# RMS norm of eight attention heads: one root and one reciprocal of 8 by 512 for all heads, spread by matmuls

## The reference

```python
def rmsnorm(x, g):
    xf = x.astype(jnp.float32)
    y = xf * lax.rsqrt(jnp.mean(xf * xf, axis=-1, keepdims=True) + EPS)
    return (y * g.astype(jnp.float32)).astype(x.dtype)

def diff_attention(q, k, v, lam, subln_g, lam_init):
    ...
        p = jax.nn.softmax(sc - slopes * dist, axis=-1)
        a = p[:, :, 0] - lam * p[:, :, 1]
        return jnp.einsum('bhqk,bkhe->bqhe', a.astype(v.dtype), v)
    ...
    o = jnp.moveaxis(o, 0, 1).reshape(b, s, DA_HEADS, DA_V_DIM)
    o = rmsnorm(o, subln_g) * (1.0 - lam_init)
    return o.reshape(b, s, DA_V_W)

def hybrid_layer(...):
    ...
    mk, mv = jnp.split(m @ w_mem_kv, 2, axis=-1)
    o_xa = memory_attention(xa_q..., mk..., mv...)
    ...
    merged = (gate[:, :, 0] * (o_da @ w_da_o)
              + gate[:, :, 1] * (o_wa @ w_wa_o)
              + gate[:, :, 2] * (o_xa @ w_xa_o))
```

## Time and profile before

| | |
|---|---|
| profiled execution | 2739.36 us |
| its span, first to last instruction | 2737.6 us |
| mean granted TensorE clock | 0.959 of full |
| busy: TensorE / weight load / VectorE / ScalarE / GpSimd | 2386.6 / 1581.4 / 948.2 / 497.2 / 1024.2 us |
| chain that ended last | TensorE 67%, DMA 13%, VectorE 12%, ScalarE 5%, issue 2% |
| HBM read | 523.56 MB, 192 GB/s over the span |
| GpSimd busy in slices 7 to 10 of 40 (the first layer's FFN) | 0.6, 0.8, 0.8, 0.8 |

### The profile page before, as it was taken

The page is one execution under the profiler, slowest core; times in us unless marked ns, Lnnn a source line. Parts: engine busy times, 40 slices in busy tenths (PEclk is TensorE's granted clock), DMA queues, the critical chain, the costliest instruction groups (busy, mean ns, idle before and its releaser), DMA issues.

```text
span 2737.6 us, 27015 instructions
## 1 busy us (share of the span) xinstructions
PE 2386.6 (87%) x11244; PEld 1581.4 (58%) x11244; DVE 948.2 (35%) x1323; ACT 497.2 (18%) x1067; POOL 1024.2 (37%) x497
## 2 busy tenths in 40 slices
PE   6999968999989988787899999599888888888886
PEld 4778837887878856565668887533323232332322
DVE  4664664555020156544732363401111101021012
ACT  2324222121010044454431010100000000000001
POOL 5444606888787744332538887200000000000000
PEclk9999989999999999898999999699999999999999
DMA  4211202322222210100213224489999999999996
GB/s 133 70 47 47 93 0 66 104 93 92 93 93 79 93 47 31 47 32 31 93 53 101 93 93 154 184 363 416 416 418 417 418 417 417 416 416 417 417 418 279
DMA packets 172341, 527.43 MB, mean 193 GB/s; under 512 B 9954, under 2 KB 92091, under 8 KB 139451
## 3 DMA queue, kind: packets, MB, share of 16 engines
q1 hardware_dynamic: 169008, 521.17, 49.1%
q10 hardware_dynamic: 3211, 4.51, 0.5%
HBM read 523.56 MB, written 2.10 MB: 192 GB/s over the span
## 4 chain that ended last, share of the span: by engine, by line
PE 67%; DMA 13%; DVE 12%; ACT 5%; issue 2%; ACTq 0%; POOL 0%; SPq 0%; DVEq 0%; POOLq 0%
PE ps L1298 9%; PE ps L1299 9%; PE ps L1300 9%; PE ps L1756 8%; PE ps L1729 7%; DMA hT<-in_w_exp_up 5%; PE ps L1451 4%; DMA arena<-in_w_exp_up 4%; DMA ring<-in_w_exp_up 4%; PE ps L1314 3%; PE ps L1315 2%; PE ps L1316 2%; PE ps L1690 2%; ACT arena L722 1%; PE ps L1714 1%
## 5 line engine op out<-in xcount | busy, mean ns | idle before, releaser
L457 POOL TENSOR_TENSOR w_hi<-ring,one 128x1024 fp32r<-128x1024 f32 x208 | 403.8, 1942 | 516.4 <-PE ps L1300 285.7
L460 POOL TENSOR_TENSOR w_lo<-ring,w_hi 128x1024 fp32r<-128x1024 f32 x222 | 543.4, 2448 | 58.0 <-ACT w_hi L773 41.6
L1298 PE MATMUL ps<-h_hi,w_hi 128*128 128x512 f32 x864 | 346.2, 401 | 8.4 <-DVE h_lo L880 5.8
L1300 PE MATMUL ps<-h_hi,w_lo 128*128 128x512 f32 x864 | 337.7, 391 | 0.0
L1299 PE MATMUL ps<-h_lo,w_hi 128*128 128x512 f32 x864 | 337.7, 391 | 0.0
L552 POOL TENSOR_TENSOR arena<-arena 128x512 f32<-128x512 f32 x8 | 8.4, 1048 | 834.6 <-PE ps L1702 796.8
L1729 PE MATMUL ps<-ring,arena 128*64 128x512 f32 x944 | 212.6, 595 | 42.6 <-DMA ring<-in_w_exp_up 41.8
L1729 PE MATMUL ps<-arena 128*64 128x512 f32 x848 | 191.9, 595 | 39.8 <-DMA arena<-in_w_exp_up 39.8
L1298 PEld LDWEIGHTS ps<-h_hi,w_hi 128*128 128x128 f32 x864 | 163.1, 189 | 50.4 <-DVE h_lo L880 6.7
L1299 PEld LDWEIGHTS ps<-h_lo,w_hi 128*128 128x128 f32 x864 | 163.2, 189 | 36.8 <-issue 4.3
L1300 PEld LDWEIGHTS ps<-h_hi,w_lo 128*128 128x128 f32 x864 | 162.9, 189 | 34.6
(11 more groups left out here) (297 smaller groups left out, 3903.4 us busy)
## 6 DMA issues: line engine op xcount, KB each, us to landing
arena<-in_w_exp_down SPq DMA_DIRECT2D x66, 1024.0 KB, 19.9
ring<-in_w_exp_gate SPq DMA_DIRECT2D x59, 1024.0 KB, 24.1
ring<-in_w_exp_up SPq DMA_DIRECT2D x59, 1024.0 KB, 25.4
arena<-in_w_exp_gate SPq DMA_DIRECT2D x53, 1024.0 KB, 21.8
arena<-in_w_exp_up SPq DMA_DIRECT2D x53, 1024.0 KB, 23.0
ring<-in_w_exp_down SPq DMA_DIRECT2D x52, 1024.0 KB, 22.0
ring<-in_w_in SPq DMA_DIRECT2D x34, 1024.0 KB, 5.1
ring<-in_ffn_w_up SPq DMA_DIRECT2D x22, 1024.0 KB, 5.1
```

Source lines behind the costliest of these rows:

```text
L457: nc.gpsimd.tensor_tensor(hi, w, one[:].unsqueeze(2).to_broadcast(list(w.shape)), ALU.mult).then_inc(w_high, 1)
L460: nc.gpsimd.tensor_tensor(lo, w, hi.bitcast(f32), ALU.subtract).then_inc(w_split, 1)
L1298: mm(o, w[0][:, k, :], h[0][:, k, 0:ntok], start=(k == 0), stop=False)
L1300: last = mm(o, w[1][:, k, :], h[0][:, k, 0:ntok], start=False, stop=(k == KT - 1))
```

## The change

The sum of squares is now gathered, not spread. `head_col` is 128 by 15 with one column of 1/128 in the middle, and a window of 8 columns from it has that column at place h. So the product of head h puts its mean on partition h of one 8 by 512 block in PSUM bank 4 and adds zero to the others; the eight heads accumulate into it. ScalarE takes one root of 8 by 512 when all eight are in, and VectorE one reciprocal of 8 by 512. Then TensorE spreads row h over 128 partitions by a product with column h of the identity, repeated 128 times (`norm_rows`), into banks 5 to 7 in turn, and VectorE's multiply reads it from PSUM. These eight products stand between the two halves of the value projection, the multiplies behind the copies of its first half. Memory attention now also waits for all eight multiplies. `mean128` and seven eighths of `ort` and `orr` are gone.

```diff
--- before.py
+++ after.py
@@ -63,9 +63,9 @@
         hT, hT_at = place(sb("hT", [P, KT, S]), KT * S)
         arena, arena_at = place(sb("arena", [P, ARENA]), ARENA)
         one = sb("one", [P, 1])
+        head_col = sb("head_col", [P, 15])
         ident = sb("ident", [P, P])
         mean64 = sb("mean64", [P, P])
-        mean128 = sb("mean128", [P, P])
         vec = sb("vec", [P, NVEC])
         wr = sb("wr", [P, KT, NE])
         epsb = sb("epsb", [P, 1])
@@ -161,7 +161,7 @@
         memt = ar(23040, 2, D)
         memn = ar(25088, 2, D)
         junkm = ar(12160, D)
-        osq, ort, orr = ar(8192, 2, S), ar(9216, 2, S), ar(10240, 2, S)
+        osq, ort, orr = ar(8192, 2, S), ar(9216, S)[0:DA_H], ar(9728, S)[0:DA_H]
         xa_q, mkT, mv = ar(18944, KT, S), ar(23040, KT, MEM), ar(25088, 2, D)
         o_xa = xa_q
         xa_p = ar(4096, 2, 4, MEM)
@@ -464,7 +464,8 @@
             nc.gpsimd.memset(ident[:], 0.0)
             nc.gpsimd.memset(mean64[:], 0.0)
             nc.gpsimd.memset(epsb[:], EPS)
-            nc.gpsimd.memset(mean128[:], 1.0 / 128)
+            link(nc.gpsimd.memset(head_col[:], 0.0))
+            nc.gpsimd.memset(head_col[:, 7:8], 1.0 / 128)
             link(nc.gpsimd.memset(mask[:], 0.0))
             link(nc.gpsimd.memset(selB[:], 0.0))
             nc.gpsimd.memset(mean64[0:64, 0:64], 1.0 / 64)
@@ -772,18 +773,13 @@
                 w = view(ring[:, c % RS, :])
                 A(w_hi[:, i % 2, :].rearrange("p (k n) -> p k n", k=w.shape[1]), w, F.Copy).then_inc(w_highA, 1)
 
-            for h in range(9):
-                if h < 8:
-                    if h >= 2:
-                        act.wait_ge(on_ps, h - 1)
-                    A(osq[:, h % 2, :], o_raw[:, h, :], F.Square).then_inc(on_sq, 1)
-                    high_part(by_act.start + h)
-                if h:
-                    m = h - 1
-                    act.wait_ge(on_ps, m + 1)
-                    if m >= 2:
-                        act.wait_ge(on_rr, m - 1)
-                    A(ort[:, m % 2, :], ps[:, 4 + m % 2, :], F.Sqrt, bias=epsb[:]).then_inc(on_rt, 1)
+            for h in range(8):
+                if h >= 2:
+                    act.wait_ge(on_ps, h - 1)
+                A(osq[:, h % 2, :], o_raw[:, h, :], F.Square).then_inc(on_sq, 1)
+                high_part(by_act.start + h)
+            act.wait_ge(on_ps, 8)
+            A(ort, ps[0:DA_H, 4, :], F.Sqrt, bias=epsb[0:DA_H]).then_inc(on_rt, 1)
             for i in by_act[8:]:
                 high_part(i)
             for u in range(XA_H + 1):
@@ -1115,22 +1111,19 @@
 
             norm(3, memt, memn)
             norm_lo(3, mem_lo, mem_hi, MEMG, MEM)
-            for h in range(9):
-                if h < 8:
-                    n = J_M + h
-                    dve.wait_ge(pj_ps, n + 1)
-                    V.tensor_copy(mkT[:, h, :], ps[:, h % 4, 0:MEM]).then_inc(pjD, 1)
-                if h:
-                    m = h - 1
-                    dve.wait_ge(on_rt, m + 1)
-                    V.reciprocal(orr[:, m % 2, :], ort[:, m % 2, :]).then_inc(on_rr, 1)
-                    dve.wait_ge(on_rr, m + 1)
-                    V.scalar_tensor_tensor(out=o_da[:, m, :], in0=o_raw[:, m, :], scalar=vec[:, SUBG:SUBG + 1],
-                                           in1=orr[:, m % 2, :], op0=ALU.mult, op1=ALU.mult).then_inc(on_done, 1)
+            for h in range(8):
+                dve.wait_ge(pj_ps, J_M + h + 1)
+                V.tensor_copy(mkT[:, h, :], ps[:, h % 4, 0:MEM]).then_inc(pjD, 1)
+            dve.wait_ge(on_rt, 1)
+            V.reciprocal(orr, ort).then_inc(on_rr, 1)
             for m in range(8, 12):
                 t, half = (m - 8) % 2, (m - 8) // 2
                 dve.wait_ge(pj_ps, J_M + m + 1)
                 V.tensor_copy(mv[:, t, half * 512:half * 512 + 512], ps[:, m % 4, :]).then_inc(pjD, 1)
+                for h in range(8) if m == 9 else ():
+                    dve.wait_ge(on_ps, 9 + h)
+                    V.scalar_tensor_tensor(out=o_da[:, h, :], in0=o_raw[:, h, :], scalar=vec[:, SUBG:SUBG + 1],
+                                           in1=ps[:, 5 + h % 3, :], op0=ALU.mult, op1=ALU.mult).then_inc(on_done, 1)
             for u in range(XA_H + 2):
                 if u < XA_H:
                     for qb in range(4):
@@ -1594,12 +1587,22 @@
             for h in range(8):
                 proj_T(1, (mem_hi, mem_lo), MEM)
                 pe.wait_ge(on_sq, h + 1)
-                if h >= 2:
-                    pe.wait_ge(on_rt, h - 1)
-                mm(ps[:, 4 + h % 2, :], mean128[:], osq[:, h % 2, :], start=True, stop=True).then_inc(on_ps, 1)
-            proj_tok((mem_hi, mem_lo), MEM // P, D)
+                mm(ps[0:DA_H, 4, :], head_col[:, 7 - h:15 - h], osq[:, h % 2, :], start=(h == 0), stop=(h == 7)).then_inc(on_ps, 1)
+
+            def norm_rows(h):
+
+                pe.wait_ge(on_rr, 1)
+                if h >= 3:
+                    pe.wait_ge(on_done, h - 2)
+                mm(ps[:, 5 + h % 3, :], ident[0:DA_H, h:h + 1].to_broadcast([DA_H, P]), orr, start=True, stop=True).then_inc(on_ps, 1)
+
+            proj_tok((mem_hi, mem_lo), MEM // P, 512)
+            for h in range(8):
+                norm_rows(h)
+            proj_tok((mem_hi, mem_lo), MEM // P, 512)
             pj_all_done(pe, J_M + 12)
-            pe.wait_ge(on_rt, 8)
+            pe.wait_ge(on_rt, 1)
+            pe.wait_ge(on_done, 8)
             for u in range(XA_H + 2):
                 if u < XA_H:
                     for qb in range(4):
```

## The result

The changed kernel takes 2742.28 us, the median of 17 runs (2733.19 to 2745.09). Beside them 17 runs of the kernel before gave 2738.11 (2730.46 to 2739.08). The ratio is 1.0020 with a 95% interval of 1.0012 to 1.0028: 4.2 us slower by the medians, 5.5 by the ratio, inside the 0.3% that I had called no change, but clear of the noise of so many runs. The forecast was 2737.0 in a range of 2729.5 to 2742.

A forecast was written before the change was run, and what follows sets the result against it. TensorE, waiting for weight halves held up by late reciprocals and roots, was taken to bound the stage. Half 12's readiness -7.2 us, eight products +6.1 (6.9 less 0.8): -1.1, from median 2738.11 to 2737.0; range 2729.5 to 2742.

The forecast's parts named there:

- the 0.3% that I had called no change: Whole kernel: about 0.3%, 8.2 us, is what a measurement can tell from no change; chance of landing within, 0.88.
- The wait of half 10 and the low clock behind it: Value weights' third half on TensorE: 6.05 us idle and 1.7 us of low clock go; it starts 5.4 us sooner.
- The sums of squares with 8 outputs cost nothing: Heads' sums on TensorE: 8 output rows instead of 128 change nothing, less than 0.1 us a head either way.
- The eight products in 6.9 us: Spreading products on TensorE between halves 11 and 12 of the weights: 0.86 us each, 6.9 us in all.
- No fall of the clock: TensorE up to memory attention: longest rest 0.6 us, so the granted clock stays at 1.00.
- The rival on the slower side: Spreading products filling 8 of 128 rows get 1.2 GHz: 13.8 us instead of 6.9, +7.5 us, 2745.6; chance 0.06.
- The slow multiplies: VectorE's eight multiplies: 2.5 to 2.9 us stalls beside GpSimd vanish with a PSUM operand; if stalled, end +0.7 instead of -1.1.
- It moves the end one for one: Stage before memory attention: everything behind waits for TensorE's counts, so what it gains or loses moves the end as much.
- The range: Whole kernel: 2729.5 to 2742 us, from the low figure to beyond the stalled multiplies, leaving out the clock's case.

The follow-up runs named there:

- e4: Kernel before, with ScalarE's high parts of halves 10 and 11 moved ahead of the roots of heads 6 and 7: 2727.61 us against 2736.43, ratio 0.9978; again 0.9973.
- e2: Changed kernel with only the sums of squares padded to 128 outputs, spreading products left at 8 partitions: 2742.47 us, ratio 1.0022 to before; stage 65.04 us.
- e7: Changed kernel with 64 outputs instead of 8 in the sums of squares; trace only: step of a head 4.06 us, stage 65.67 us.
- e3: Changed kernel with only the spreading products padded to 128 partitions, sums left at 8 outputs: 2737.16 us, ratio 1.0001 to before; stage 61.77 us.
- e5: Changed kernel with the spreading products over 64 partitions instead of 8; trace only: last sum to memory attention 33.98 us, stage 62.11 us.
- e6: Changed kernel with the spreading products over 32 partitions instead of 8; trace only: last sum to memory attention 38.85 us, stage 66.99 us.
- e1: Changed kernel with sums of squares and spreading products both padded to full 128: 2736.83 us against 2736.43 before, ratio 1.0010; stage 59.83 us.
- e8: Changed kernel with its eight spreading products two by two ahead of halves 12 to 15; trace only: last sum to memory attention 33.80 us, stage 61.94 us.

## Why the prediction was wrong

The forecast was a gain of 1.1 us; the stage lost 5.9.

- *The wait of half 10 and the low clock behind it* (13.0 us behind the last sum, to become 7.6): right, 7.7. e4 shows it alone. VectorE's busy time fell by 34 us (948.2 to 914.2), and what that gave TensorE is this one wait and the low clock in it.
- *The sums of squares with 8 outputs cost nothing, less than 0.1 us a head*: wrong, 0.29 us a head, 2.3 in all. The step failed because I took the length of a record (592 ns with 64 outputs) for its price; it stayed so (594 ns with 8 outputs, 590 before), and the loss is between records. e2 takes the loss away, e7 shows that 64 outputs have it too. The trace of the kernel before had it to see, where full products are followed by some over 64 partitions in differential attention; the step into them is 0.32 us, that between the full ones 0.23:

```profile
1024.56 0.39 PE L1487 MATMUL ps<-h_lo,w_hi 128*128 128x512 f32 x1
1024.79 0.39 PE L1488 MATMUL ps<-h_hi,w_lo 128*128 128x512 f32 x1
1025.11 1.99 PE L1507 MATMUL ps<-arena 64*128 64x512 f32 x8
```

- *The eight products in 6.9 us*: the size was wrong, 9.5 us. At the full clock one follows the other after 0.86 us, as forecast (e3, and 0.87 in e5); five of the sixteen records ran at half of it.
- *No fall of the clock*, since the longest rest is 0.6 us: wrong, and with the 2.6 us above this is the larger part. The rest was 0.90 us, but the clock fell in the products, without a rest. Behind them it cost 2.4 us more: from half 12 to half 14 it took 9.19 us, not the 6.81 from 1358.36 to this row of before:

```profile
1365.17 0.50 PE L1314 MATMUL ps<-w_hi,mem_hi 128*128 128x512 f32 x1 [0.99 <-POOL w_lo L460]
```

  The rival on the slower side had the mechanism, "the clock falls in the products", with +7.5; I gave it 0.06. What I held against it, full clock at 64 partitions, is true, and says nothing of 8: the turn lies between 32 and 64 (e5, e6, one trace each). From there the sum is -1.1 + 2.3 + 2.6 + 2.4 = +6.2, and 5.9 was measured; between the first sum and the last lie only seven of the eight steps.
- *The slow multiplies* won't be met in PSUM form: right. In the changed kernel the first five stand in one row of 4.18 us, one every 0.86, while GpSimd was on a low part from 1353.34 to 1355.69; the other three took 0.75 each. TensorE never waited for a bank.
- *It moves the end one for one*: right within 1 us. Memory attention starts 5.5 us later (the stage's 5.9, with 0.4 less ahead of it), and the span is 4.6 us longer.
- *The range*: 2742.0 at its top left out a rival that I had priced at 2745.6.

The Trainium skill (TensorE: Matmul & The Clock Gate, Part 1) tells of the clock as an answer to how busy TensorE is and names rests as what lowers it. That fits the kernel before, where the clock fell within the rest of 6.05 us (0.91 from 1346 to 1347, 0.50 from 1347 on). It does not fit the changed one, where TensorE was busy 10.00 of 10.00 us from 1347 to 1357 and the granted clock fell all the same; the measurement decides.

## What to carry to other kernels

When work moves to TensorE in a new shape, price the seams and not the record: look for the step before and behind a product of another shape in the same trace, and keep the shape of the neighbours by padding with zeros. The padding itself cost TensorE nothing here (3.73 us a head and 0.86 us a product); look also at what else the padding brings, since the first key block was 2.1 us slower in every kernel with padded sums. Don't put products over few partitions in one long piece; padding them to 64 or more, or full ones between them, kept the clock here. And before work is rebuilt to shorten a wait, ask which single instruction it released: here a change of order on ScalarE took 6.5 us off the stage without the new work.

## What the runs showed of the hardware

- TensorE's granted clock fell to 1.2 GHz in the middle of gapless products over 8 partitions (in the changed kernel, e2, e7) and over 32 (e6), and not over 64 or 128 (e5, e1, e3). In the changed kernel it was low for 10 us and came back at about 1366.7, in the full products behind.
- Two such products over 8 partitions between pieces of 2.9 us of full ones left it at 1.00 (e8).
- A product with 8 or 64 outputs among products with 128 costs 0.3 us more than one with 128 (4.02 and 4.06 against 3.73 us a head), though its weight load is shorter (87 and 134 ns against 190). In the changed kernel's trace the loads at the seams start with their matmuls and not under those in front.
- A reciprocal of 8 by 512 takes 3.34 us, as one of 128 by 512 (3.34 to 3.35): fewer partitions did not shorten it.
